# The experts' up products as three float32r products of split operands

## What is computed

```python
xs = jnp.take(xt, top_i, axis=0)
hid = jax.nn.silu(jnp.einsum('ecd,edf->ecf', xs, w1)) * jnp.einsum('ecd,edf->ecf', xs, w3)
ye = jnp.einsum('ecf,efd->ecd', hid, w2) * top_v[..., None].astype(h.dtype)
out = jnp.zeros((n, D), h.dtype).at[top_i.reshape(-1)].add(ye.reshape(-1, D))
```

## Time and profile before

| | |
|---|---|
| median of three runs | 3073.3 us |
| the profiled execution's own time | 3072.36 us |
| its span, first to last instruction | 3069.4 us |
| mean granted TensorE clock | 0.971 of full speed |
| PE busy | 2890.4 us (94%) |
| DVE / ACT busy | 1137.7 us (37%) / 785.5 us (26%) |
| experts' up products, PE busy | 567.6 us, 4096 matmul records |
| experts' down products, PE busy | 286.8 us, 2048 matmul records |

### The profile page before, as it was taken

One profiled execution on the slowest core, in us unless ns is written; L12 is line 12 of the kernel. 1 busy time (PEld: TensorE's weight loads), 2 busy tenths in 40 slices (PEclk: granted clock), 3 DMA queues, 4 the chain that ended last, 5 costly groups with the idle time before them and its releaser, 6 DMA issues.

```text
span 3069.4 us, 36418 instructions
## 1 busy us (share of the span) xinstructions
PE 2890.4 (94%) x14849; PEld 2210.8 (72%) x14849; DVE 1137.7 (37%) x2067; ACT 785.5 (26%) x1677; POOL 202.8 (7%) x263
## 2 busy tenths in 40 slices
PE   7999799999999999999998999984999999999993
PEld 1444377777788475757576886542999999999993
DVE  1346655555343335363634434448011111111113
ACT  1311344444333314141413331332111111111111
POOL 1111000000000001010101000000000100000003
PEclk9999899999999999999999999996999999999996
DMA  9300000000010000001000011326577787777855
GB/s 301 132 28 28 28 1 0 0 0 0 28 55 14 5 28 21 28 21 28 21 28 32 28 55 67 149 87 246 198 261 251 250 280 237 271 244 247 284 181 216
DMA packets 177806, 336.25 MB, mean 110 GB/s; under 512 B 16340, under 2 KB 38356, under 8 KB 177654
## 3 DMA queue, kind: packets, MB, share of 16 engines
q1 hardware_dynamic: 168180, 307.86, 28.3%
q0 software_dynamic: 7392, 26.22, 3.6%
q10 hardware_dynamic: 2084, 0.06, 0.0%
HBM read 301.09 MB, written 33.03 MB: 109 GB/s over the span
## 4 chain that ended last, share of the span: by engine, by line
PE 87%; DVE 5%; ACT 2%; DMA 2%; issue 2%; POOL 1%; SPq 0%; POOLq 0%; DVEq 0%; ACTq 0%; PEldq 0%
PE ps L217 20%; PE ps L1958 18%; PE ps L817 14%; PE ps L1976 8%; PE ps L635 6%; PE ps L659 5%; PE ps L644 3%; PE ps L1039 2%; PE ps L292 1%; PE ps L1103 1%; PE ps L1120 1%; DMA RW<-in_w_mod_dram 1%; PE ps L1099 1%; DVE R L1729 1%; DVE R L1728 1%
## 5 line engine op out<-in xcount | busy, mean ns | idle before, releaser
L217 PE MATMUL ps<-RW,R 128*128 128x256 f32 (+1 forms) x2080 | 642.6, 463 | 0.9 <-DVE R L1635 0.9
L1958 PE MATMUL ps<-RW,R 128*128 128x160 f32 x4096 | 567.6, 300 | 1.9 <-ACTq L2011 1.9
L1958 PEld LDWEIGHTS ps<-RW,R 128*128 128x128 f32 x4096 | 560.6, 191 | 2.3 <-ACTq L2011 2.3
L217 PEld LDWEIGHTS ps<-RW,R 128*128 128x128 f32 x2080 | 386.7, 190 | 210.9 <-issue 181.3
L1976 PE MATMUL ps<-WK,R 128*128 128x160 f32 x2048 | 286.8, 299 | 0.0
L2075 DVE TENSOR_TENSOR WK<-WK,ps 128x160 f32<-128x160 f32 x128 | 41.1, 321 | 660.3 <-PE ps L1958 660.3
L1976 PEld LDWEIGHTS ps<-WK,R 128*128 128x128 f32 x2048 | 280.1, 190 | 0.0
L817 PE MATMUL ps<-W_high,tile_high 128*128 128x512 f32 x640 | 251.0, 392 | 7.8 <-DVE W_low L884 7.8
L817 PE MATMUL ps<-W_high,tile_low 128*128 128x512 f32 x640 | 250.5, 391 | 0.0
L817 PE MATMUL ps<-W_low,tile_high 128*128 128x512 f32 x640 | 250.5, 391 | 0.0
L635 PE MATMUL ps<-R,WK 128*128 128x512 f32 (+1 forms) x416 | 188.4, 586 | 6.8 <-DVE R L705 2.7
(11 more groups left out here) (237 smaller groups left out, 2761.4 us busy)
## 6 DMA issues: line engine op xcount, KB each, us to landing
R<-in_w_dram SPq DMA_DIRECT2D x96, 2048.0 KB, 10.3
RW<-in_w_mod_dram SPq DMA_DIRECT2D x12, 2048.0 KB, 9.9
RW<-in_w_in_dram SPq DMA_DIRECT2D x7, 2048.0 KB, 7.7
RW<-in_w_in_dram SPq DMA_DIRECT2D x8, 1024.0 KB, 7.2
x_scratch<-WK SPq DMA_DIRECT2D x10, 512.0 KB, 2.6
xhat_scratch<-WK SPq DMA_DIRECT2D x10, 512.0 KB, 3.7
ffn_scratch<-WK SPq DMA_DIRECT2D x10, 512.0 KB, 4.9
R<-x_scratch SPq DMA_DIRECT2D x1, 5120.0 KB, 15.7
```

The costliest lines, as they stand in the source:

```text
L217: m = pe.matmul(out, lhs(k), Wslot[slot][:, k, off:off + width], start=(k == 0), stop=(k == KD - 1))
L1958: m = pe.matmul(bank(4 + 2 * a + f % 2, CAP), We[a][:, k, f * P:(f + 1) * P], xe[:, e % GE, k, :], start=(k == 0), stop=(k == KD - 1))
```

## The change

The 2048 up products each become three float32r products into the same PSUM block: high weights with high rows, high weights with low rows, low weights with high rows. The operands are split on the way. For each f and a, ScalarE copies the weight block of all eight k (128x1024) into a float32r slot of a ring of eight (four f, two a), and VectorE writes the difference in place over the float32 weights. The 160 rows of an expert are split in the same way, once per expert (128x1280 elements). The ring and the row parts take the SBUF room of `xe`, `xgc`, `xgl`, `sl` and `yoc`, which move elsewhere. The split runs four blocks f ahead of PE: the first four of the next expert during the down products, the last four behind the silus of the first four. The context rows of a group are turned one expert earlier. SP's and POOL's DMAs keep their places, except for the context gathers, which come up to three experts earlier.

```diff
+        We_low = [w.rearrange("p (k n) -> p k n", k=KD) for w in (R1r[:, 0:8 * D], R2r[:, 2 * D:10 * D])]
+        RING = 4
+        We_high = [RWr[:, (2 + n) * D:(3 + n) * D] for n in range(6)] + [R3r[:, (8 + n) * D:(9 + n) * D] for n in range(2)]
+        We_high = [w.rearrange("p (k n) -> p k n", k=KD) for w in We_high]
+        W_SPLIT, X_SPLIT = 2 * 4 * KD, 2 * 4 * NT
+
+        def column(w, f):
+            return w[:, :, f * P:(f + 1) * P]
+
+        def high_of(f, a):
+            return We_high[2 * (f % RING) + a]
...
-            def slots_ready(e):
-                pe.wait_ge(S("slots_kept_act"), slots_before(e + 1))
-                pe.wait_ge(S("slots_kept_dve"), slots_before(e + 1))
-
             def up(e):
-                slots_ready(e)
+                pe.wait_ge(S("tile_split"), X_SPLIT + e + 1)
                 for f in range(KD):
-                    if f % 4 == 0:
-                        for a in range(2):
-                            pe.wait_ge(S(f"expert_landed{a}{f // 4}"), e * 16 + 16)
                     for a in range(2):
                         if a == 0 and e * KD + f >= 2:
                             pe.wait_ge(S("hidden_made"), e * KD + (f - 1))
+                        pe.wait_ge(S("weights_split"), W_SPLIT + (e * KD + f) * 2 + a + 1)
+                        high, low = high_of(f, a), column(We_low[a], f)
                         for k in range(KD):
-                            m = pe.matmul(bank(4 + 2 * a + f % 2, CAP), We[a][:, k, f * P:(f + 1) * P], xe[:, e % GE, k, :], start=(k == 0), stop=(k == KD - 1))
+                            for n, (w, x) in enumerate(((high, 0), (high, 1), (low, 0))):
+                                m = pe.matmul(bank(4 + 2 * a + f % 2, CAP), w[:, k, :], x_parts[x][:, k, :], start=(k == 0 and n == 0), stop=(k == KD - 1 and n == 2))
                         m.then_inc(S(f"up_done{a}"), 1)
...
+            def split_slots(e):
+                act.wait_ge(S("slots_kept_dve"), slots_before(e) + 1 if e else 2)
+                if e:
+                    act.wait_ge(S("up_done1"), e * KD)
+                act.activation(x_parts[0], xe[:, e % GE, :, :], ACT.Copy).then_inc(S("tile_high"), 1)
+
+            def weights_high(e, f):
+                for a in range(2):
+                    act.wait_ge(S(f"expert_landed{a}{f // 4}"), e * 16 + 16)
+                    if e * KD + f >= RING:
+                        act.wait_ge(S(f"up_done{a}"), e * KD + f - RING + 1)
+                    act.activation(high_of(f, a), column(We[a], f), ACT.Copy).then_inc(S("weights_high"), 1)
...
+                    if f + RING < KD:
+                        weights_high(e, f + RING)
...
+                    if e + 1 < NE and d == 2:
+                        split_slots(e + 1)
+                    if e + 1 < NE and 3 <= d < 3 + RING:
+                        weights_high(e + 1, d - 3)
+                    if (e + 2) % GE == 0 and e + 2 < NE and d == 5:
+                        keep_ctx_slots((e + 2) // GE)
...
+            for f in range(RING):
+                weights_high(0, f)
             keep_slots(0)
             keep_ctx_slots(0)
+            split_slots(0)
             for e in range(NE):
...
+            def split_slots(e):
+                dve.wait_ge(S("tile_high"), X_SPLIT + e + 1)
+                dve.tensor_tensor(x_parts[1], xe[:, e % GE, :, :], x_parts[0].bitcast(F32), ALU.subtract).then_inc(S("tile_split"), 1)
+
+            def weights_low(e, f):
+                for a in range(2):
+                    dve.wait_ge(S("weights_high"), W_SPLIT + (e * KD + f) * 2 + a + 1)
+                    dve.tensor_tensor(column(We_low[a], f), column(We[a], f), high_of(f, a).bitcast(F32), ALU.subtract).then_inc(S("weights_split"), 1)
...
+                    if f + RING < KD:
+                        weights_low(e, f + RING)
+
+            dve.wait_ge(S("ffn_cleared"), 16 * NT)
+            for f in range(RING):
+                weights_low(0, f)
             keep_slots(0)
             keep_ctx_slots(0)
+            split_slots(0)
             for e in range(NE):
                 hidden(e)
                 if e + 1 < NE:
                     keep_slots(e + 1)
-                if e + 1 < NE and (e + 1) % GE == 0:
-                    keep_ctx_slots((e + 1) // GE)
+                    split_slots(e + 1)
+                    for f in range(RING):
+                        weights_low(e + 1, f)
+                        if (e + 2) % GE == 0 and e + 2 < NE and f == 2:
+                            keep_ctx_slots((e + 2) // GE)
```

More of the change, by code:

```diff
@@ L95, in build_program, with both @@
         ps = ctx.enter_context(nc.psum_tensor("ps", [P, 8 * BANK], F32))
[L96 to L99, removed]
+        def both(name, n):
+            with nc.sbuf_tensor(name, [P, n], F32) as plain:
+                pass
+            return plain, sb(name + "r", [P, n], F32R)
+        R1, R1r = both("R1", NT * D)
+        R2, R2r = both("R2", NT * D)
+        R3, R3r = both("R3", NT * D)
+        RW, RWr = both("RW", 2 * KD * BLK)
         WORK_N = 12304
@@ L1811, in build_program @@
         NG, GE = NE // 4, 4
-        xgl = [work(D, at=64), work(D)]
-        sl = [work(CAP) for _ in range(2)]
+        sl = [carry[:, n * CAP:(n + 1) * CAP] for n in range(2)]
+        x_parts = [W.rearrange("p (k c) -> p k c", k=KD) for W in
+                   (Wsplit[0][:, :, :].rearrange("p k n -> p (k n)")[:, 64 + n * KD * CAP:64 + (n + 1) * KD * CAP] for n in range(2))]
+        xgl = [R1[:, 8 * D:9 * D], R1[:, 9 * D:10 * D]]
+        xe = work(GE * KD * CAP, at=64 + 2 * KD * CAP).rearrange("p (e k c) -> p e k c", e=GE, k=KD)
         hid = work(KD * CAP).rearrange("p (k c) -> p k c", k=KD)
@@ L1816, in build_program, with ctx_slots_before @@
         yTc = work(KD * GE * CAP_CTX).rearrange("p (k c) -> p k c", k=KD)
-        yol, yoc = work(D), work(D)
-        xe = RW[:, 2 * D:2 * D + GE * KD * CAP].rearrange("p (e k c) -> p e k c", e=GE, k=KD)
-        xgc = RW[:, 7 * D:8 * D]
+        yol = work(D)
+        xgc, yoc = R2[:, 0:D], R2[:, D:2 * D]
+        We_low = [w.rearrange("p (k n) -> p k n", k=KD) for w in (R1r[:, 0:8 * D], R2r[:, 2 * D:10 * D])]
[7 more added lines that the diff above has]
+            return We_high[2 * (f % RING) + a]
+        def ctx_slots_before(g):
+            return (GE + 1) * g if g else 1
         def slots_before(e):
-            return e + (e + GE - 1) // GE
+            return sum(1 for x in range(NE) if x < e) + sum(1 for g in range(NG) if (GE * g if g else 1) <= e)
         FLUSH = ((0, 1, 2, 3), (4, 5, 6, 7), (8, 9, 10, 11), (12, 13, 14), (15,))
@@ L1893, in pool_moe @@
                     gather(e + 1)
-                if e % GE == 0 and e < NE:
-                    gather_ctx(e // GE)
+                if e % GE == 1 and e // GE + 1 < NG:
+                    gather_ctx(e // GE + 1)
                 add_back(e - 1)
@@ L1979, in down @@
                         turn_slots(e + 1, d)
-                    if e + 1 < NE and (e + 1) % GE == 0 and 3 <= d < 5:
-                        turn_ctx_slots((e + 1) // GE, d - 3)
+                    if (e + 2) % GE == 0 and e + 2 < NE and 3 <= d < 5:
+                        turn_ctx_slots((e + 2) // GE, d - 3)
             for s in range(2):
@@ L2006, in keep_ctx_slots @@
             def keep_ctx_slots(g):
-                act.wait_ge(S("slots_turned"), 2 * slots_before(GE * g) + 3)
+                act.wait_ge(S("slots_turned"), 2 * ctx_slots_before(g) + 1)
+                if g:
+                    act.wait_ge(S("tile_split"), X_SPLIT + GE * g)
                 for k in range(4):
@@ L2050, in keep_ctx_slots @@
             def keep_ctx_slots(g):
-                dve.wait_ge(S("slots_turned"), 2 * slots_before(GE * g) + 4)
+                dve.wait_ge(S("slots_turned"), 2 * ctx_slots_before(g) + 2)
+                if g:
+                    dve.wait_ge(S("tile_split"), X_SPLIT + GE * g)
                 for k in range(4, 8):
```

7 lines of the change are left out of this document (3 added, 4 removed).

## The result

| | before | changed |
|---|---|---|
| median | 3073.7 us (four runs) | 3244.2 us (four runs, 3238.5 to 3245.6) |
| profiled execution, its span | 3072.4, 3069.4 us | 3244.1, 3242.3 us |
| ratio | | 1.055, 95% interval 1.0532 to 1.0568 |

The changed kernel is 5.5% slower. The forecast was 3211 us with a range of 3160 to 3306.

The account below looks back on a forecast made before the run. The prediction took TensorE's rate to bound the experts: 2048 up products at +64.3 ns give +131.7 us, the start +6, so +138 on 3072.4 is 3210, as a median 3211 us; range 3160 to 3306.

Parts of the forecast that it names:

- The load as the term that decides: Up products: loading each 128-column stationary block outlasts the 66 ns stream, so float32r products come 112 ns apart.
- The sum for PE: Up products on TensorE: three of 112 ns for one of 271.7, +64.3 ns times 2048, +131.7 us.
- The extra 13 ns: Unexplained extra of a 512-column float32r product; left out of the 112 ns distance, used only for the upper bound.
- rival 1: Up products: float32r load gets out of the way, stream decides, 83 ns a product, 3033 us; chance 0.10.
- Splits at 0: ScalarE's copies and VectorE's differences in the experts stay hidden behind PE: 0 us, +15 us at most.
- DMAs at 0: Up weights must land earlier, 4 MB needing 11 us in about 20 us: hidden, 0.
- start at +6: Before the first up product VectorE must make eight differences, so it starts at 2151.5 to 2152, not 2145.87: +6 us.
- The low end of the range: Whole kernel: 3073 + 89 + 4 = 3166 us, from a 105 ns load; drawn wider to 3160.
- Rival 3: Up products: the granted clock falls to 1.2 GHz, load twice as long, 224 ns a product, 3900 us; chance 0.03.
- 125 ns a product: Up products: upper bound if float32r's additional 13 ns comes on top of 112, +212 us.
- rival 2: Up products: float32r at 160 columns runs like float32, 271.7 ns each, +1113 us, 4192 us; chance 0.07.

Follow-up runs that it names:

- the splits alone: Changed kernel with all copies, differences and waits, but PE makes the 2048 float32 up products of unsplit weights with high rows: 3077.1 us, ratio 1.0012.

## Why the prediction was right, and where it was not

- **The load as the term that decides: right.** The slope of the load times over their columns, read in the trace of before, gave 105 ns, the narrowest float32 products 112 as a distance; measured 111.6. The runs with 64, 160 and 256 columns and the float32 run with 64 show a distance that no stream explains, that does not depend on the columns up to 160, that goes by the clock and that is the same for both types.
- **What is argued in it.** No run gives the up products a narrower stationary block, so that the 111.6 ns are the load, and not a fixed price of every product, rests on the load times over their columns. The trace of before speaks against a fixed price: just ahead of the experts PE turns sixteen small pieces, with stationary blocks of 32 columns, in 0.39 us with 0.194 for one, 13 ns apart and at half clock. Those blocks have 16 rows and not 128, so the point stays open by that much:

```profile
2131.36 0.39 PE L1767 MATMUL ps<-ident,R 16*32 16x4 f32 x16 [15.33 <-DVEq L1740]
```

- **The sum for PE: right**, 128.6 us for 131.7.
- **The extra 13 ns: right to keep it out of the value.** It exists (118.3 ns with 256 columns), and does not show with 160. The working read the 512-column distance a little too long (229.7 ns for 226.7 at full clock), which moves only rival 1, from 83 to 81 ns.
- **Splits at 0, DMAs at 0, start at +6: right.** 5.4 us in the profiles of the changed kernel and of the splits alone, whose time rose by some 4. (The low end of the range took 4 us for the start without a reason.)
- **The clock: the mis-judged step.** Rival 3 stood at 0.03 because "the clock stays at full speed in all stages where PE has short pauses and loads". This looked at phases entered at full clock and not at the one entered after idling: the earlier trace rows show 0.50 at 2120 to 2130, and the first up phase follows. Nor did the clock fall, as the rival had it; it failed to rise, and in one phase of sixteen. It cost 38.6 us (37.0 in the up phase, 1.6 behind it), which is the whole miss: 3211 - 3 for the load at 111.6 + 38.6 = 3247, measured 3244. That the measured time lies in the range is luck: the range was open on that side for 125 ns a product, which the runs exclude, and not for the clock.
- **Rival 1, a load that gets out of the way, and rival 2, float32r as slow as float32 when narrow: both wrong.** Distances of 83 and 271.7 ns were to show them.

By the Trainium skill, TensorE: Matmul & The Clock Gate, section Weight-path perf modes, a fast load is on for 128 weights whose type is not FP32; these runs show none for float32r, with a distance of 111.6 ns, for 111.4 in float32. The same page, section LDWEIGHTS (loading the stationary operand), gives the columns over 1.2, by which a load of 128 columns is estimated at 106.7 ns; at full clock the distances of the runs agree to 5 ns, and at half clock they do not (212.8 ns).

## What to carry to other kernels

In these runs a product costs the longer of its stream (with its fixed part) and the load of the next stationary block, and a type that is four times faster shortens only the stream. Count the loads before replacing one product by three: at 160 columns three float32r products cost 335 ns against 272 of one float32 product, and with two loads (one product of 320 columns, one of 160) 258. Where a phase comes after idling, look at the clock over all of it: here it stayed at half for 82 us with PE never idle. And before a few microseconds between two medians are put down to an edit, look in the traces where they lie.

## What the runs showed that was not expected

- PE without idle is not the same as PE at full clock. With float32r products of 64 columns the clock fell from full to half in each later up phase (2300 to 2600: 0.60 on average); with 160 columns it stayed at full in fifteen phases and at half for 82 us in the first; with 256 columns, and with 320 and 160, it rose within the first phase (48.4 us for 384 products). Float32 products of 64 columns stayed at half through the first phase and at full through the later ones.
- A float32r product has 12 to 13 ns on top of its stream at full clock: 118.3 ns with 256 columns, 226.7 with 512. At half clock the 512 columns came 426 ns apart (ten distances from 797.13 to 801.39), which is their stream alone. A float32 pass has 2.5 (135.8 ns for 320 cycles, which take 133.3). What it is stays open.
- VectorE's differences of 1024 elements follow each other at 1.14 us, though each record is 1.22 us long.
